# Expert rows shared between VectorE and PE by running clocks, tile 2's experts chosen in three parts, and the sample's drains moved behind the first choice

## What is computed

```python
q = (xf @ p['peer_wq']).astype(f32).reshape(n, PEER_HEADS, 2, PEER_HALF)
s1 = jnp.einsum('nhd,hkd->nhk', q[:, :, 0], p['peer_k1'].astype(f32))
s2 = jnp.einsum('nhd,hkd->nhk', q[:, :, 1], p['peer_k2'].astype(f32))
v1, i1 = lax.top_k(s1, PEER_TOPK)
v2, i2 = lax.top_k(s2, PEER_TOPK)
...
sc, sel = lax.top_k(cand, PEER_TOPK)
idx = jnp.take_along_axis(cidx, sel, axis=-1)
gate = jax.nn.softmax(sc, axis=-1)
...
h = jnp.einsum('nhkd,nd->nhk', peer_u[ii], xi)
a = jax.nn.gelu(h.astype(f32), approximate=False) * gi
return jnp.einsum('nhk,nhkd->nd', a.astype(x.dtype), peer_v[ii])
```

## Time and profile before

| | us |
|---|---|
| median of 3 runs | 2005.94 |
| the three runs | 2003.02, 2005.94, 5541.88 |
| the profiled execution's own time | 2001.23 |
| its span, first to last instruction | 1999.3 |
| busy in the span | PE 1600.5, DVE 1305.9, ACT 426.0, POOL 1217.5 |
| DMA | 675.07 MB, mean 338 GB/s over the span |

### The profile page before, as it was taken

One profiled execution on the slowest core, in us unless ns is written; L12 is line 12 of the kernel. 1 busy time (PEld: TensorE's weight loads), 2 busy tenths in 40 slices (PEclk: granted clock), 3 DMA queues, 4 the chain that ended last, 5 costly groups with the idle time before them and its releaser, 6 DMA issues.

```text
span 1999.3 us, 16829 instructions
## 1 busy us (share of the span) xinstructions
PE 1600.5 (80%) x4873; PEld 793.3 (40%) x4873; DVE 1305.9 (65%) x3087; ACT 426.0 (21%) x1018; POOL 1217.5 (61%) x1370
## 2 busy tenths in 40 slices
PE   7889976978999797793778787868787777777776
PEld 5588735545555453341233232323232323222222
DVE  7742135998778788859496777655777645444444
ACT  2123201145333231311121121121121112111111
POOL 0055004665647665655777777777777776777771
PEclk9889897999999999897989998989988998999999
DMA  6254137898889999988999999999999999999995
GB/s 221 106 109 145 53 129 256 315 392 326 316 308 367 406 387 352 386 286 287 351 409 409 409 409 409 409 410 409 409 409 409 409 409 410 409 409 409 409 409 230
DMA packets 186554, 675.07 MB, mean 338 GB/s; under 512 B 20960, under 2 KB 23440, under 8 KB 186048
## 3 DMA queue, kind: packets, MB, share of 16 engines
q0 software_dynamic: 167056, 609.25, 79.0%
q1 hardware_dynamic: 17632, 59.51, 8.3%
q10 hardware_dynamic: 1776, 5.24, 0.7%
HBM read 669.71 MB, written 3.69 MB: 337 GB/s over the span
## 4 chain that ended last, share of the span: by engine, by line
DMA 30%; PE 24%; DVE 24%; POOL 12%; issue 8%; ACT 1%; ACTq 0%; DVEq 0%; POOLq 0%
DMA region<-in_pu,region 15%; DMA wring<-in_pu,region 8%; PE bank L965 7%; POOL region L637 4%; DVE region L1427 4%; PE bank L860 4%; POOL region L628 3%; POOL wring L628 3%; DMA wring<-in_pv,region 3%; DVE wring L1427 2%; PE first_banks L860 2%; DMA region<-in_pv,region 2%; DMA small<-in_pv,region 2%; PE first_banks L917 2%; PE bank L917 1%
## 5 line engine op out<-in xcount | busy, mean ns | idle before, releaser
L965 PE MATMUL bank<-region,small 128*128 128x512 f32 (+1 forms) x1392 | 675.1, 625 | 169.5 <-ACT small L1710 118.7
L637 POOL DMA_INDIRECT region<-in_pv,region x392 | 388.8, 992 | 180.9 <-issue 98.2
L965 PEld LDWEIGHTS bank<-region,small 128*128 128x128 f32 (+1 forms) x1392 | 253.6, 193 | 571.2 <-issue 421.7
L628 POOL DMA_INDIRECT region<-in_pu,region x298 | 309.5, 1039 | 187.5 <-issue 73.1
L1427 DVE CUSTOM_DVE_ANT_0 wring<-wring,first_banks 128x1024 f32<-128x1024 f32 x228 | 276.1, 1220 | 211.5 <-DMA wring<-in_pu,region 210.8
L628 POOL DMA_INDIRECT wring<-in_pu,region x278 | 278.2, 1001 | 105.9 <-issue 64.9
L1427 DVE CUSTOM_DVE_ANT_0 region<-region,first_banks 128x1024 f32<-128x1024 f32 x156 | 189.3, 1220 | 145.4 <-DMA region<-in_pu,region 144.7
L1710 ACT ACTIVATE small<-small,region 128x128 f32<-128x128 f32 (+1 forms) x514 | 165.3, 386 | 370.6 <-DVE region L1399 343.1
L1427 DVE CUSTOM_DVE_ANT_0 region<-region 128x1024 f32<-128x1024 f32 x142 | 171.8, 1226 | 43.3 <-DMA region<-in_pu,region 42.2
L1718 ACT ACTIVATE region<-region 128x4 f32<-128x4 f32 x144 | 29.6, 205 | 729.3 <-DVE region L1427 729.1
L965 PE MATMUL bank<-discretisation,small 128*128 128x512 f32 (+1 forms) x200 | 113.0, 693 | 83.8 <-ACT small L1710 74.7
(11 more groups left out here) (345 smaller groups left out, 1930.8 us busy)
## 6 DMA issues: line engine op xcount, KB each, us to landing
wring<-in_w SPq DMA_DIRECT2D x100, 512.0 KB, 6.7
region<-in_pv,region POOLq DMA_INDIRECT x392, 13.5
region<-in_pu,region POOLq DMA_INDIRECT x298, 11.1
wring<-in_pu,region POOLq DMA_INDIRECT x278, 16.9
region<-in_w SPq DMA_DIRECT2D x4, 512.0 KB, 7.8
out_y<-region ACTq DMA_DIRECT2D x4, 512.0 KB, 6.6
small<-in_small ACTq DMA_DIRECT2D x1, 1669.0 KB, 8.3
xT<-in_xT SPq DMA_DIRECT2D x1, 1536.0 KB, 12.5
```

The costliest lines, as they stand in the source:

```text
L628: pool.indirect_dma_start(ring_u[u_at.place[q]], None, io["pu"], bass.IndirectOffsetOnAxis(ind[:, k:k + 1], 0)).then_inc(g_u[u_at.place[q] ...
L637: pool.indirect_dma_start(ring_v[v_at.place[q]], None, io["pv"], bass.IndirectOffsetOnAxis(ind[:, k:k + 1], 0)).then_inc(g_v[v_at.place[q] ...
L965: last = mm(bank[6 + hf][0:tn, :], diag[:, d % DIAGS, 0:tn], ring_v[v_at.place[q]][:, 512 * hf:512 * hf + 512], start=k == 0, stop=t > 1 a ...
```

## The change

In `CHOICES` tile 2 gets the parts of tile 1: heads 0-1, 2-3, 4-7. So `mix` ends with two tops, a choose and an index of two heads instead of four, with one more "wait" item (4.0 in the cost table, no instruction) ahead of them. The rest, in `late`, is two tops, a choose and an index at every half step from 2 to 5 of tile 2, then four tops, a choose and an index at every second half step from 6; the third part's scores (PE) are asked for behind top 3. SPREAD goes from 176 to 184.

In the list at the start both sample halves keep their place as PE products, but the two `drain_wo` items move behind the first index, just ahead of the sample's layer norm.

`on_vector` is computed by a new function from the finished list. It walks DVE's own order and PE's own order, keeps a clock for each that is never ahead of the arrival of U rows (2.6 us a slot, at most four half steps in flight, 4 us to land), and gives a row to DVE if DVE's clock plus 1.29 is below PE's plus 1.95, at the half step in which the row is executed, four slots behind its dot.

```diff
--- before.py
+++ after.py
@@ -37,18 +37,21 @@
 
 V_LAG = {1: 4, 0: 4, 2: 4, 3: 4, 4: 4}
 
-SPREAD = 176
+SPREAD = 184
 CHOSEN_FROM, CHOSEN_TO = 50, 112
 
 COST = {"top": (5.0, 0), "choose": (4.6, 0), "index": (5.0, 0), "sc": (0, 2.5), "s": (4.1, 1.0), "p": (2.8, 0), "pt": (0, 1.4),
         "pv": (0.4, 1.6), "qkv": (2.4, 10.3), "turn": (0, 1.2), "gs": (0, 5.5), "ga": (0, 5.5), "merge": (2.2, 8.2), "wo": (0, 3.5), "wo_last": (0, 7.0), "drain_wo": (0.7, 0),
-        "ln": (6.2, 0), "xt": (0, 1.3), "wq": (0.3, 5.5), "fold": (0, 0), "wait": (4.0, 0)}
+        "ln": (6.2, 0), "xt": (0, 1.3), "wq": (0.3, 5.5), "fold": (0, 0), "wait": (4.0, 0), "final": (7.0, 0)}
 DOT, V_BY_VECTOR, V_BY_TENSOR = 1.31, 1.29, 1.95
+
+SLOT, LANDING, IN_FLIGHT = 2.6, 4.0, 4
+VECTOR_BEHIND = {"qkv": 2, "s": 1, "p": 1, "pv": 1, "merge": 2, "drain_wo": 1, "ln": 1}
 DIAGS = 8
 STEP_SLOTS = 4
 HALF_STEP = 2
 
-CHOICES = {1: [(0, 2), (2, 4), (4, 8)]}
+CHOICES = {1: [(0, 2), (2, 4), (4, 8)], 2: [(0, 2), (2, 4), (4, 8)]}
 AHEAD = 2
 AHEAD_PLACES = 7
 
@@ -90,8 +93,8 @@
     s += [("pt", 0, 1), ("pv", 0, 1)] + [("ups", 0, m) for m in range(8)] + [("y", 0), ("y", 1), ("ht",)]
     s += [("merge", 0, m) for m in range(8)]
     wo = lambda t, hf: [("wo_last", t, hf), ("drain_wo", t, hf)]
-    s += wo(1, 0) + wo(1, 1) + [("ln", 1)] + wo(0, 0) + [("xt", 1)] + [("wqf", h) for h in range(AHEAD)] + [("sc", 1, 0)] + wo(0, 1)
-    s += [("top", 1, 0), ("top", 1, 1), ("choose", 1, 0), ("index", 1, 0), ("ln", 0), ("xt", 0)] + [("wql", h) for h in range(AHEAD)]
+    s += wo(1, 0) + wo(1, 1) + [("ln", 1), ("wo_last", 0, 0), ("xt", 1)] + [("wqf", h) for h in range(AHEAD)] + [("sc", 1, 0), ("wo_last", 0, 1)]
+    s += [("top", 1, 0), ("top", 1, 1), ("choose", 1, 0), ("index", 1, 0), ("drain_wo", 0, 0), ("drain_wo", 0, 1), ("ln", 0), ("xt", 0)] + [("wql", h) for h in range(AHEAD)]
     s += [("wq", 0, 2), ("wq", 0, 3), ("sc", 1, 1)] + [("wq", 0, h) for h in range(4, 8)]
 
     first = [[("top", 1, 2)], [("top", 1, 3)], [("choose", 1, 1), ("sc", 1, 2)], [("index", 1, 1)]]
@@ -114,22 +117,20 @@
     mix += [[("drain_wo", 2, 0), ("drain_wo", 2, 1), ("wo_last", 4, 0)], [("ln", 2)], [("wo_last", 4, 1)]]
     mix += [[("drain_wo", 3, 0), ("drain_wo", 3, 1)], [("ln", 3)], [("drain_wo", 4, 0), ("drain_wo", 4, 1), ("xt", 2)], [("ln", 4)], [("xt", 3)]]
     mix += [[("wait",)], [("xt", 4)], [("wait",)]] + [[("wq", 1, h)] for h in range(8)]
-    mix += [[("sc", 2, 0), ("sc", 2, 1)]] + [[("top", 2, h)] for h in range(4)] + [[("choose", 2, 0)], [("index", 2, 0)]]
+    mix += [[("sc", 2, 0), ("sc", 2, 1)], [("wait",)]] + [[("top", 2, h)] for h in range(2)] + [[("choose", 2, 0)], [("index", 2, 0)]]
     tops = [[("top", 0, h)] for h in range(4)] + [[("choose", 0, 0), ("sc", 0, 1)], [("index", 0, 0)]]
     tops += [[("top", 0, h)] for h in range(4, 8)] + [[("choose", 0, 1)], [("index", 0, 1), ("fold",)]]
 
     cost = lambda entry: sum(sum(COST[i[0]]) for i in entry)
     rate = sum(cost(e) for e in mix + tops) / SPREAD
-    slots, placed, d_load, p_load, on_vector = 0, 0.0, 0.0, 0.0, set()
+    slots, placed = 0, 0.0
     for t in ORDER[:2]:
         for c in range(n_slots(t) // HALF_STEP):
             s.append(("peer", t, c))
             if c == 1 and t != ORDER[0]:
                 s.append(("final", ORDER[0]))
-                d_load += 8.7
-            for k in range(HALF_STEP * c, HALF_STEP * c + HALF_STEP):
+            for k in range(HALF_STEP):
                 slots += 1
-                d_load += DOT
                 entries = []
                 if tops and slots >= CHOSEN_FROM + (CHOSEN_TO - CHOSEN_FROM) * (12 - len(tops)) // 11:
                     entries.append(tops.pop(0))
@@ -137,18 +138,12 @@
                     entries.append(mix.pop(0))
                 for entry in entries:
                     placed += cost(entry)
-                    d_load += sum(COST[i[0]][0] for i in entry)
-                    p_load += sum(COST[i[0]][1] for i in entry)
                     s += entry
-                if k and d_load + V_BY_VECTOR < p_load + V_BY_TENSOR:
-                    on_vector.add((t, k))
-                    d_load += V_BY_VECTOR
-                else:
-                    p_load += V_BY_TENSOR
         s.append(("last", t))
     assert not mix and not tops
 
-    late = [("top", 2, h) for h in range(4, 8)] + [("choose", 2, 1), ("index", 2, 1)]
+    late = [[("top", 2, 2)], [("top", 2, 3), ("sc", 2, 2)], [("choose", 2, 1)], [("index", 2, 1)]]
+    late += [[("top", 2, h)] for h in range(4, 8)] + [[("choose", 2, 2)], [("index", 2, 2)]]
     for t in ORDER[2:]:
         s.append(("banks", t))
         nxt = [("sc", t + 1, 0), ("sc", t + 1, 1)] + [("top", t + 1, h) for h in range(4)] + [("choose", t + 1, 0), ("index", t + 1, 0)]
@@ -157,14 +152,14 @@
             s.append(("peer", t, c))
             if c == 1:
                 s.append(("final", ORDER[ORDER.index(t) - 1]))
-            if late and c >= 2 and c % 2 == 0:
-                s.append(late.pop(0))
+            if late and c >= 2 and (c < 6 or c % 2 == 0):
+                s += late.pop(0)
             elif not late and t < 4 and c >= 8 and c % 3 == 2 and nxt:
                 s.append(nxt.pop(0))
         assert t == 4 or not nxt
         s.append(("last", t))
     s.append(("final", ORDER[-1]))
-    return s, on_vector
+    return s
 
 
 def mixer_first(items):
@@ -206,6 +201,38 @@
         else:
             out.append(item)
     return out + [h[1] for h in held]
+
+
+def rows_on_vector(items):
+
+    steps = [(t, c) for t in ORDER[:2] for c in range(n_slots(t) // HALF_STEP)]
+    load = []
+    for engine, order in enumerate((half_steps_behind(items, VECTOR_BEHIND), mixer_first(items))):
+        sums, n = [0.0] * (len(steps) + 1), -1 + engine
+        for item in order:
+            if item[0] == "peer" and item[1] not in ORDER[:2]:
+                break
+            if item[0] == "peer":
+                n += 1
+            elif n >= engine:
+                sums[min(n, len(steps))] += COST.get(item[0], (0, 0))[engine]
+        load.append(sums)
+    out, vector, tensor, came, done = set(), 0.0, 0.0, 0.0, []
+    for n, (t, c) in enumerate(steps):
+        came = max(came + HALF_STEP * SLOT, done[n - IN_FLIGHT] + LANDING if n >= IN_FLIGHT else 0.0)
+        vector = max(vector, came) + HALF_STEP * DOT
+        tensor = max(tensor + load[1][n], came)
+        ready = c * HALF_STEP - STEP_SLOTS
+        last = c + 1 == n_slots(t) // HALF_STEP
+        for k in range(max(0, ready), ready + HALF_STEP + (STEP_SLOTS if last else 0)):
+            if k and vector + V_BY_VECTOR < tensor + V_BY_TENSOR:
+                out.add((t, k))
+                vector += V_BY_VECTOR
+            else:
+                tensor += V_BY_TENSOR
+        vector += load[0][n]
+        done.append(max(vector, tensor))
+    return out
 
 
 def item_jobs(item):
@@ -267,7 +294,8 @@
 
 
     def __init__(self):
-        self.items, self.on_vector = schedule()
+        self.items = schedule()
+        self.on_vector = rows_on_vector(self.items)
         self.filled, self.drained, self.before, self.bank = {}, {}, {}, {}
         self.passed, self.index, self.pieces, self.last_use = {}, {}, [], {}
         scores = self.items.index(("sc", ORDER[0], 0))
@@ -1450,7 +1478,7 @@
                     "s": do_s, "p": do_p, "pv": do_pv, "ups": do_ups, "merge": do_merge, "drain_wo": do_drain_wo, "ln": do_ln, "top": do_top, "choose": do_choose,
                     "index": do_index,
                     "peer": do_peer, "last": do_last, "final": do_final}
-            for item in half_steps_behind(plan.items, {"qkv": 2, "s": 1, "p": 1, "pv": 1, "merge": 2, "drain_wo": 1, "ln": 1}):
+            for item in half_steps_behind(plan.items, VECTOR_BEHIND):
                 if item[0] in here:
                     here[item[0]](*item[1:])
 
```

## The result

The changed kernel takes 1980.97 us (median of 4 runs, 1977.35 to 1984.62) against 2005.22 of the kernel before: 0.9881 of its time, 95% interval 0.9867 to 0.9894. That is 24 us, 1.2%, inside the range of the prediction (1935 to 1988) and of its sign, but "within 2%" where "faster" had the larger chance, and 24 us where the sum said 40. One of the four runs of the kernel before took 5541.88 us; it counts as slow and isn't in the ratio. The profiled execution took 1979.38 us with a span of 1977.6.

A forecast was written before the change was run, and what follows sets the result against it. The prediction took saturated DMA gathers (409 GB/s) to bound the kernel's end, so gains before 985 us count in full; its terms summed to 40.3 us off 2001.2, so 1961 us, range 1935 to 1988.

The forecast's parts named there:

- the sum: Whole kernel: 6.3 + 4 + 2 + 9 + 10 + 12 - 1 - 2 = 40.3 us gained, so 1961 us.
- What bounds the kernel: DMA saturated at 409 GB/s late in the kernel; gains before 985 us come off the end one for one.
- Term 1: Start: sample drains behind the first choice bring the first gather to about 301.8 us; 6.3 us kept.
- Term 2: SPREAD 176 to 184 thins the work per slot: 4 us in 345-510, 2 us in 650-850.
- Term 3: V rows by running clocks: 9 us in 510-650, 10 in 850-905, some 15 to 20 more rows on VectorE.
- Term 4: Tile 2 chosen in three parts: 12 us in 905-985, bounds 5 and 21.5; 1 us lost after 985.
- Term 5: GpSimd's own pace in 309-985 us: about 20 more V rows at 0.17 us each, 2 us lost.
- rival (b): GpSimd takes the place: added VectorE rows stretch its issues, 21 us instead of 2, so 1980; chance 0.09.
- Rival (a): Planner's clocks assume 2.6 us a slot, the stage has 3.5; the rows' 19 us are gone: 1980; chance 0.17.
- Rival (d): Slower: in-order V-row waits on VectorE, 345 to 850 us, cost 78 us against 40 gained: 2039; chance 0.04.
- Rival (c): Nearly all idle DMA between 510 and 985 us is recovered: 1921 to 1945; chance 0.18.
- the signs named: First gather about 302 us; 510-650 above 360 GB/s; 75 to 82 V rows on VectorE; wq products: VectorE above 70%.

The follow-up runs named there:

- the control: The changed kernel run again without any edit on the chip of the experiments: 2098.46 us, 0.9877 of the kernel before.

## Why the prediction was right or wrong

- **What bounds the kernel.** Right. From slot 192 on the gain nearly stays as it is (24.8 us, 22.9 at slot 264, and 21.7 in the span), at 409 GB/s from 1100 us on. The kernel's time is where saturation begins.
- **Term 1, the head start (6.3 us).** The work was right: 7.5 us at slot 0 on the second chip, 2.8 in the first pair. What failed is "of 7.7 us 6.3 are kept" and, behind it, "anything gained before 985 us comes off the end one for one". As the dots show it, it doesn't hold ahead of stretches that have waits of their own. By slot 120 1.3 us were left, in one profile each; the times can't tell.
- **Term 2, the spread (4 and 2 us).** The stretch 345-510 gave 4.1, as forecast, but not by the spread as far as the runs show: from dot 0 to dot 56 the control takes 203.0 us, the two kernels at SPREAD 176 take 202.8 and 202.9. That agreement is luck. The 2 us for 650-850, with "bounds 0 and 8", is the step that failed worst: it lost 7.3 us. I had priced the spread as a smooth thinning, though it moves entries past fixed events. I did not look for what the last merge and `wo` would meet six slots later, at the change of tiles, although had this stretch with both engines at 81%. The row moved on PE takes the wait of 14.4 us away and SPREAD 176 shortens it to 6.0 and 9.0; the row alone brings 9 to 12 us. What the stretch lost ahead of that wait, between dots 120 and 128, stays open.
- **Term 3, the rows (9 and 10 us).** About 14 us by two removals, 21 alone. The sum of 19 is near, the count was wrong: 7 more rows, not 15 to 20. 510-650 gave 6.5 with PE still at 133.8 of 140 and VectorE at 119.2. In 850-905 the balance that I worked out didn't happen. I had all 8 rows between the wq products on VectorE; six of them are still on PE. Since the wq products stand eight slots later now, these are the rows of slots 154 to 159, which the old sums had on VectorE and the new function puts on PE. The eight products with the rows between them took 56.6 us before (845.5 to 902.1) and take 52.9 now, all of it busy on PE. That is 3.7 us, two rows of 1.78, where I took 10. If 850-905 gave 10.3 us all the same, as by the limits of the slots, the agreement is luck. Both the count and these rows could have been read off the list that the new function returns.
- **Term 4, tile 2 (12 us, -1 behind).** 11.5 or 6.0 in the trace, by the limits, and -1.7 behind; 8 us by the removal at 176. The direction and the bounds (5 to 21.5) hold, the 12 was too much if anything. The margin that I gave GpSimd's queue held: 404 GB/s in 960-1100.
- **Term 5 and rival (b).** GpSimd's mean issue in the stage rose from 1.10 us (385 issues) to 1.13 (392), about 10 us spread over a stage in which it waits more than 100. Not the bound. The rule of the Trainium skill (SBUF — State Buffer, Who interferes with whom) says that a VectorE instruction with two SBUF inputs contends with a GpSimd instruction that reads SBUF; the direction fits (1.10 to 1.13 us), and no run here separates its share.
- **Rival (a), the balance stays on paper:** its time, 1980, is the one that came, its reason isn't. The rows did pay; the spread took part of it back. **Rival (d):** VectorE's waits for V rows rose from 14.7 to 34.3 us, but the kernel without them gained nothing up to slot 144 and was slower behind it, so no cost of theirs is shown. **Rival (c)** stays the upper end: 96 of 115 us of idle DMA are still there.
- **The sum.** The parts as removed give 13 to 15 us (rows), 8 (tile 2), about 0 (drains) and -1 to -6 (spread): some 15 to 22, against 26 by the ratio on that chip and 24 in the first pair. They don't add up exactly, and need not: each was taken out with the others in place. Of the signs named, the rows (69, not 75 to 82), the first gather (305.3 us, not 302), GB/s above 360 in 510-650's place (355) and VectorE above 70% in the wq products (32.7 of 52.9 us, 62%) all fell short. That showed a balance smaller than the one summed up, before any experiment.

Open: which pairing of entries makes the 11 us by slot 56 in two kernels, and what SPREAD 184 loses between dots 120 and 128; no run isolates either. Row order and SPREAD 176 together weren't tried.

## What to carry to other kernels

Where a list of items is spread over slots, a factor is no smooth knob: look up which items land next to a fixed event (a change of tiles, a row that only one engine can take), and what queues in order behind their waits. A head start ahead of stretches with waits of their own need not be a gain until the last of them is passed; read it at the point where the bound sets in. And to test such an event, move one item on one engine: an edit that changes the sum of costs moves everything.

## What the runs showed of the hardware that was not expected

The same program with the same bytes ran 6% slower in the experiments than in the first pair: there, gathers in the last stretch don't reach 409 GB/s. The control in 1100-1500 and 1500-1900 us:

```profile
1100.00:1500.00 400.00, 281.46 (x607) 117.61 (x606) 251.00 (x651) 62.61 (x187) 267.66 (x282) 0.87 0.97 369
1500.00:1900.00 400.00, 281.72 (x577) 113.95 (x575) 219.55 (x475) 63.03 (x190) 261.74 (x276) 0.86 0.95 363
```

The sixteen DMA engines are nearly as busy (0.95 to 0.97 against 1.03) and move a tenth less, 363 to 369 GB/s. From dot 0 to dot 120 the control was 3% slower than the changed kernel in the first pair (407.9 against 396.5 us), from dot 192 to the last 11% (1097.9 against 990.7). So most of the difference is the rate in saturation; all twelve profiles of the experiments show it (362 to 375 GB/s). Why isn't shown: another chip, or something else that drew on the same memory, would look alike here. The granted clock was lower too (0.87 and 0.86 against 0.94 in the earlier trace rows), but PE was busy only 70% of these stretches. The change's ratio came out the same, 0.9877 and 0.9881.
